# The opening of a two-layer hybrid diffusion backbone on one NeuronCore: another order of loads, statistic and modulation vectors, and three smaller moves

## What is computed

```
mx = split(silu(c)     @ ada_w[l] + ada_b[l], 9)     # shift, scale, gate for 3 sub-layers
mc = split(silu(c_ctx) @ ada_w[l] + ada_b[l], 9)
def ffn_sublayer(t, shift, scale, gate, g_pre, g_post, w_in, w_out):
    y = swiglu(rms_norm(t, g_pre) * (1 + scale) + shift, w_in, w_out)
    return t + 0.5 * gate * rms_norm(y, g_post)
lam = exp(sum(dl[0]*dl[1])) - exp(sum(dl[2]*dl[3])) + lambda_init     # used by attention a
kv  = rms_norm(parts[7]) @ w_ukv;  q = rms_norm(parts[6]) @ w_uq      # the norms of the latents
```

## Time and profile before

| | before |
|---|---|
| median of 3 runs | 2849.93 us |
| the profiled execution: its time | 2852.55 us |
| the profiled execution: its span | 2850.5 us |
| PE busy | 2737.2 us, 96% of the span |
| DVE / ACT / POOL busy | 61% / 44% / 9% |
| mean granted TensorE clock | 0.982 |

### The profile page before, as it was taken

The page is one execution under the profiler, slowest core; times in us unless marked ns, Lnnn a source line. Parts: engine busy times, 40 slices in busy tenths (PEclk is TensorE's granted clock), DMA queues, the critical chain, the costliest instruction groups (busy, mean ns, idle before and its releaser), DMA issues.

```text
span 2850.5 us, 42837 instructions
## 1 busy us (share of the span) xinstructions
PE 2737.2 (96%) x15754; PEld 2295.3 (81%) x15754; DVE 1743.1 (61%) x2907; ACT 1251.5 (44%) x2227; POOL 248.6 (9%) x342
## 2 busy tenths in 40 slices
PE   6999999999889999999999999999999989998997
PEld 4888898886666776788888898888988677877997
DVE  5677456656745443358676386772778766636754
ACT  2222355226545534446322354223553556555443
POOL 0000000111210000011000000100102120001000
PEclk8999999999999999999999999999999989999999
DMA  6555357431111121145555355553565222414654
GB/s 235 172 189 199 107 155 244 133 103 38 38 45 39 59 76 61 47 153 171 163 190 171 113 174 185 188 193 96 172 199 190 77 75 68 144 60 148 235 173 130
DMA packets 106643, 385.48 MB, mean 135 GB/s; under 512 B 12289, under 2 KB 14081, under 8 KB 104193
## 3 DMA queue, kind: packets, MB, share of 16 engines
q1 hardware_dynamic: 86370, 303.82, 33.1%
q0 software_dynamic: 20128, 79.70, 8.5%
HBM read 379.27 MB, written 4.20 MB: 135 GB/s over the span
## 4 chain that ended last, share of the span: by engine, by line
PE 85%; DVE 9%; ACT 3%; issue 2%; DMA 1%; POOL 0%; SPq 0%; POOLq 0%; DVEq 0%; ACTq 0%
PE ps L1934 24%; PE ps L1935 23%; PE ps L1942 23%; PE ps L917 3%; PE ps L896 3%; PE ps L879 2%; DVE wlo L1474 2%; PE ps L1998 1%; PE ps L2000 1%; PE ps L1995 1%; PE ps L869 1%; DVE mx L767 1%; ACT prob L683 1%; PE ps L875 1%; DVE work L1633 1%
## 5 line engine op out<-in xcount | busy, mean ns | idle before, releaser
L1474 DVE TENSOR_TENSOR wlo<-raw,whi 128x1024 fp32r<-128x1024 f32 x572 | 695.0, 1223 | 444.1 <-ACT whi L1166 443.4
L1934 PE MATMUL ps<-xhi,whi 128*128 128x512 f32 (+1 forms) x2432 | 827.8, 354 | 16.3 <-DVE xlo L1643 16.3
L1935 PE MATMUL ps<-xlo,whi 128*128 128x512 f32 (+1 forms) x2432 | 818.8, 351 | 0.0
L1166 ACT ACTIVATE whi<-raw 128x1024 fp32r<-128x1024 f32 x572 | 604.7, 1057 | 484.6 <-PE ps L1942 444.8
L1934 PEld LDWEIGHTS ps<-xhi,whi 128*128 128x128 f32 x2432 | 466.4, 192 | 85.5 <-DVE xlo L1643 18.6
L1935 PEld LDWEIGHTS ps<-xlo,whi 128*128 128x128 f32 x2432 | 467.3, 192 | 57.1
L1942 PE MATMUL ps<-xhi,wlo 128*128 128x512 f32 (+1 forms) x2432 | 509.8, 352 | 0.0
L1942 PEld LDWEIGHTS ps<-xhi,wlo 128*128 128x128 f32 x2432 | 403.7, 192 | 58.2 <-issue 0.7
L1710 DVE SCALAR_TENSOR_TENSOR work<-ada,work 128x1024 f32<-128x1024 f32 x256 | 299.4, 1220 | 2.1 <-DMA ada<-in_ada_rows 2.0
L1934 PE MATMUL ps<-ghi,whi 128*128 128x256 f32 (+1 forms) x968 | 279.0, 315 | 1.9 <-ACT whi L1166 1.9
L1935 PE MATMUL ps<-glo,whi 128*128 128x256 f32 (+1 forms) x968 | 277.9, 313 | 0.0
(11 more groups left out here) (209 smaller groups left out, 3322.9 us busy)
## 6 DMA issues: line engine op xcount, KB each, us to landing
raw<-in_ffn_in SPq DMA_DIRECT2D x192, 512.0 KB, 4.8
ada<-in_ada_rows POOLq DMA_DIRECT2D x128, 512.0 KB, 4.5
raw<-in_merge SPq DMA_DIRECT2D x96, 512.0 KB, 3.7
raw<-in_ffn_out SPq DMA_DIRECT2D x88, 512.0 KB, 3.6
raw<-in_ffn_out SPq DMA_DIRECT2D x44, 384.0 KB, 3.2
raw<-in_v_a SPq DMA_DIRECT2D x32, 512.0 KB, 4.4
raw<-in_qk_a SPq DMA_DIRECT2D x32, 512.0 KB, 3.7
raw<-in_wo SPq DMA_DIRECT2D x24, 512.0 KB, 4.0
```

What stands on the lines that cost most here:

```text
L1166: act.activation(whi[:, g.ring(SPLIT), :], raw[:, g.ring(RAW), :], ACT.Copy).then_inc(hi_ready, 1)
L1474: dve.tensor_tensor(wlo[:, g.ring(SPLIT), :], raw[:, g.ring(RAW), :], whi[:, g.ring(SPLIT), :].bitcast(F32), ALU.subtract).then_inc(lo_rea ...
L1934: pe.matmul(o, w, hi[:, first + c, ph.span], start=start, stop=False)
L1935: pe.matmul(o, w, lo[:, first + c, ph.span], start=False, stop=False)
```

## The change

1. **Loads.** Scale weights come in eight pieces, `x` in two. The order on SP is scale 0, 1, shift pair 0, scale 2, 3, half of `x`, scale 4, half of `x`, scale 5 to 7, biases and norm weights, the store of the conditioning rows, shift pairs 1 to 3, weight groups. Eight small constants and the two `ada` blocks are issued by POOL, once the last shift pair has landed.
2. **PE.** One shift pair goes ahead of the statistic, three behind it, each pair into a bank of its own. The lambda product moves to the start of the first output phase.
3. **DVE.** The newton steps follow the scale vector at once; each shift pair gets its bias when it is due (`shift_biased`); the low part of group 0 stands behind the first two `scaled`; the small constants stand behind the last `xlo`. ACT makes `whi` of group 0 behind the inverse root.
4. **Attention a.** POOL multiplies all tiles of a block with one tensor_tensor whose second operand is broadcast. The norm of the latents is spread over all eight tiles of the gate, one DVE segment a tile.
5. **The end.** The last norm uses the four instructions of the half norms (128x4x256), and each half of the output is sent as soon as it is there.

```diff
@@ pool_attention
-                    for t in range(nq // P):
-                        part = yraw[:, b % 2, t * P:(t + 1) * P]
-                        last = pool.tensor_scalar(part, part, yfac[:, b % 2, t:t + 1], None, ALU.mult)
-                    last.then_inc(done["yscaled"], 1)
+                    rows = nq // P
+                    part = yraw[:, b % 2, 0:nq].rearrange("p (t c) -> p t c", t=rows)
+                    factors = yfac[:, b % 2, 0:rows].unsqueeze(2).to_broadcast([P, rows, P])
+                    pool.tensor_tensor(part, part, factors, ALU.mult).then_inc(done["yscaled"], 1)
@@ sync
+            load_scale_w(0)
+            load_scale_w(1)
             load_shift_w(0)
+            load_scale_w(2)
+            load_scale_w(3)
+            load_x(0)
+            load_scale_w(4)
+            load_x(1)
+            for block in range(5, KC):
+                load_scale_w(block)
+            sp.dma_start(ada_b[:, :, :, :, :], io["ada_b"]).then_inc(biases_loaded, 16)
+            sp.dma_start(norm_g[:, :, :, :, :], io["norm_g"]).then_inc(biases_loaded, 16)
+            sp.wait_ge(silu_rows_made, 2)
+            sp.dma_start(silu_rows, c_all[0:1, :]).then_inc(silu_rows_stored, 16)
+            for pair in range(1, KC // ADA_PAIR):
                 load_shift_w(pair)
...
-            sp.wait_ge(done["x"], residual(plan[-1], KC - 1))
-            sp.dma_start(out, x[:, :, 0:S]).then_inc(stored, 16)
-            sp.wait_ge(stored, 16)
+            for b in range(BATCHES):
+                some = slice(b * KC // BATCHES, (b + 1) * KC // BATCHES)
+                sp.wait_ge(done["x"], base(plan[-1], "x") + b + 1)
+                sp.dma_start(out[:, some, :], x[:, some, 0:S]).then_inc(stored, 16)
+            sp.wait_ge(stored, 16 * BATCHES)
@@ gpsimd
+            pool.wait_ge(shift_w_loaded[-1], 16)
+            small = [(dlam, "dlam"), (subg, "subg"), (lat_g, "lat_g"), (cos, "cos"), (sin, "sin"), (ident, "ident"),
+                     (mask, "mask")]
+            for dst, name in small:
+                pool.dma_start(dst[tuple([slice(None)] * len(dst.shape))], io[name]).then_inc(consts_loaded, 16)
@@ latents_high (ACT)
+                for tile in range(HEAD):
+                    yield
+                    c = {2: 0, 3: 1, 4: 2, 5: 3, 6: 4}.get(tile)
+                    if c is not None:
...
                     yield
@@ scalar, norm
+                        inverse(STAT, ph.span, D, base(ph, "xsum") + KC, "xsum")
                         if not ph.post:
                             split_hi(Idx(0, 0, 0))
-                        inverse(STAT, ph.span, D, base(ph, "xsum") + KC, "xsum")
                         for c in range(KC):
+                            if not ph.post:
+                                act.wait_ge(shifts_made, c // ADA_PAIR + 1)
                             normed_high(ph, c)
@@ vector
+            def shift_biased(pair):
+
+                some = slice(pair * ADA_PAIR, (pair + 1) * ADA_PAIR)
+                dve.wait_ge(first_shift, pair + 1)
+                src = ps[:, SHIFT_BANKS[pair], 0:2 * ADA_PAIR].rearrange("p (c n) -> p c n", n=2)
+                dve.tensor_tensor(mods[:, 0, 0, some, :], src, ada_b[:, 0, 0, some, :], ALU.add)\
+                   .then_inc(shifts_made, 1)
+
+            def small_constants():
+
+                dve.wait_ge(consts_loaded, 128)
...
+                        if not ph.pre:
+                            for b in range(BATCHES):
+                                residual_added(ph, b)
+                            continue
...
                     if ph.pre:
+                        newton(step, dve, base(ph, "inv") + (2 if ph.post else 1), STAT, ph.span, D)
                         if not ph.post:
-                            split_lo(Idx(0, 0, 0))
-                        newton(step, dve, base(ph, "inv") + (2 if ph.post else 1), STAT, ph.span, D)
+                            dve.wait_ge(silu_rows_stored, 16)
                         scaled(ph, 0)
                         scaled(ph, 1)
+                        if not ph.post:
+                            shift_biased(0)
+                            split_lo(Idx(0, 0, 0))
                         for c in range(KC):
                             if c + 2 < KC:
                                 scaled(ph, c + 2)
+                                if not ph.post and c % ADA_PAIR == 0:
+                                    shift_biased(c // ADA_PAIR + 1)
+                            if not ph.post:
+                                dve.wait_ge(shifts_made, c // ADA_PAIR + 1)
                             normed_low(ph, c)
@@ tensor
-                        shift_products(range(KC - ADA_PAIR))
+                        shift_products(range(ADA_PAIR))
...
-                        shift_products(range(KC - ADA_PAIR, KC))
+                        for first in range(ADA_PAIR, KC, ADA_PAIR):
+                            shift_products(range(first, first + ADA_PAIR))
```

124 lines of the change are left out of this document (62 added, 62 removed).

## The result

The changed kernel takes 2816.53 us (median of 4 runs, 2812.94 to 2820.38), the kernel before 2852.31 on the same chip: a ratio of 0.988, 95% interval 0.9865 to 0.9896. That is 35.8 us, where 29.5 were forecast. The profiled execution took 2812.94 us, its span is 2811.3; against the span of before the gain is 39.2.

What follows compares the result with a forecast made beforehand. PE, busy 2737 of 2850.5 us, bounds the kernel; the opening is bound by bytes, then DVE. Gains 19.8 + 2.0 + 4 + 4 - 0.3 = 29.5 us gave a forecast of 2820 us, own range 2812 to 2828.

Steps and rivals of the forecast that it cites:

- The loads came in the queue's order: Opening: loads served in queue order, shift pair 0 landing at 10.6 us; rival that order fails, 2835 us, chance 0.03.
- DVE's path: Opening: newton at 28.8 us against 51.85, last `xlo` at 46.3 us, 21.2 us earlier.
- The pairs: Opening, PE: three shift pairs behind the statistic take 3.6, 5.3 and 7.0 us, ending at 43.3.
- The shift pairs are late next, not DVE: Opening: PE's first 16 passes end at 50.2 us, DVE alone would allow 47.2; opening gains 19.8 us.
- The constants: Opening: small constants from POOL land about 45.7 us, wanted at 46.3, cost 0; rival of late constants 2879 us, chance 0.01.
- The end: Last norm and output: four longer instructions and two output transfers gain 2.0 us, bounds 0.5 and 2.2.
- GpSimd's step: Attention a, POOL: one two-input instruction of 1.35 us replaces 3.4 us a block; gain 4 us, at most about 6, worst -5.
- The rival of the held-up DVE: Attention a: GpSimd's longer instruction holds up DVE, attention gives nothing or loses; 2830 us, chance 0.20.
- The latents' norm: Attention a: spreading it over eight gate tiles gains 4 us, a sixth of 27 us lost; bounds -3 and 12.
- the 0.3 for the lambda product: First output phase, PE: the moved lambda product stands between two full phases and costs 0.3 us.
- the four terms: Predicted gains: opening 19.8, end 2.0, attention a's POOL step 4 and latents' norm 4 us.
- everything fits: Rival: DVE's path decides the opening and attention gives 15 us; 2811 us, chance 0.13.

Runs made afterwards that it cites:

- u_both: Changed kernel with both attention a edits undone (POOL's single instruction per block, the spread of the latents' norm): 2829.99 us, ratio 0.9928 to the kernel before.
- u_pool: Changed kernel with GpSimd's edit undone, a block's tiles again multiplied in four (layer 1: two) one-input instructions: 2823.39 us, ratio 0.9911 to the kernel before.
- x_warmlo: Changed kernel with six products added among shift pairs 1 to 3 and group 0's low part moved to GpSimd: 2817.02 us, ratio 0.9900 to the kernel before.
- x_warm: Changed kernel with six added 128x256 products, two in each of shift pairs 1 to 3: 2819.80 us, ratio 0.9907 to the kernel before.

## Why the prediction was right, and where it was not

**The loads came in the queue's order: right.** They were about 1.1 us later than counted from the first shift pair on (11.7 instead of 10.6). The sums began at 7.7 instead of 7.4 and waited once, 1.26 us instead of 0.6, so newton began at 29.76 instead of 28.8.

**DVE's path: right.** Newton to the last `xlo` took 18.1 us; 15.65 + 1.2 + 0.7 = 17.55 were counted, and the wait for pair 3 is the other half microsecond.

**The pairs: right, one by one.** They took 3.63, 5.32 and 6.96 us, where 3.6, 5.3 and 7.0 were taken; with their overlaps that is 15.64 in all. They were meant to end at 43.3 and did at 43.7. The clock dropped at 33.4 us, inside the second, as assumed. That the profiled execution hit 5.32 is in part luck: in `u_both` the drop came at 31.2 and the same pairs ended at 46.5.

**"The shift pairs are late next, not DVE": right by 0.9 us, not by the 3 between 50.2 and 47.2.** All 16 passes were put at 0.43 us; the clock came back at 47 us, after eight of them, and the rest took 0.23 (chain above). Low passes from 48.95 instead of 50.2, while DVE was 1.6 us later than predicted, which took up most of the slack. The opening gave 20.6 us; the forecast was 19.8. Over the seven profiles with this opening the first `yinv` of layer 0 comes at 649.3 to 653.1 us, against 670.0 and 670.8 in the two with the old one, so the gain is 17 to 21.5 us and 19.8 lies inside.

**The constants: right.** No wait at 47.81.

**The end: 2.4 us, predicted 2.0 and at most 2.2.** DVE's part was as said. The output's second half took less time than the rows for transfers of 512 KB gave: the span ends 3.4 us behind the end of DVE's last instruction (2807.9), issue included.

**GpSimd's step: the mechanism right, the size not.** 4 us were taken, within -5 and 6; undoing it costs 7 to 9. "At most about 6 of the 7.5" held for the direct wait (5.8), and PE's idle time as a whole moves by 3.4, near the 4; but the term left out the clock, PE's busy time being 3.2 us higher in `u_pool`. One wait of 2.1 us was left, where none over 1.5 was foreseen. The instruction took 1.04 us in seven of the eight blocks of layer 0 (1.35 predicted) and 0.61 to 1.67 in layer 1. Two-input instructions of the same shape without a broadcast take 1.27 us at the least, so a broadcast operand has no price here. The Trainium skill's GPSIMD Engine Reference (4.1, Engine selection) would have had the two-input form cost more; against it stand 1.04 us for 128x512 in one instruction and 2.35 to 3.97 for four one-input ones in `u_pool`.

**The rival of the held-up DVE: there, but small.** DVE is busy 88.84 us in attention a of layer 0 with the one instruction, 86.59 with the four; in layer 1 56.85 against 55.13. That is 4 us of DVE in all, not 17. The two `ya` sums of 1.34 us that gave the price are there before and after, beside GpSimd's `yalo` and not beside this step; the change added one of 0.70. PE waited for GpSimd in one place only: its instruction took 1.95 us beside a low part, and PE waited 2.1. What can happen shows in `x_warmlo`: 0.88 to 4.04 us. SBUF — State Buffer of the Trainium skill (Who interferes with whom) has a port pair held for a whole instruction, by the engine that issues first. The row agrees in part: DVE's step ended only 0.3 us behind GpSimd's instruction, but by the records DVE had begun first, and its loss of 3.2 us is more than that instruction's 2.37. No run explains the difference.

**The latents' norm: mis-sized.** 4 us taken, 7 to 9 measured, within -3 and 12. I had the clock's 3.4 and 6.8 us in the sum of losses and then took a sixth of it all. The clock doesn't come back by sixths: in layer 0 the mean goes from 0.96 to 0.99 with both edits.

**Not in the sum at all: 2.8 us behind attention a of layer 0**, where the clock was at 0.88 and is now at 1.00. `u_both` has the stretch again (448.15 us to the next table load), and the kernels with one of the two edits don't (445.54 and 445.39). But that isn't proof that the edits decide it, for `x_warm` has both edits and the stretch too, 448.17 us to the next table load:

```profile
783.82:813.20 29.38, 25.53 (x139) 16.78 (x138) 16.89 (x44) 15.88 (x44) 0.00 (x0) 0.88 0.06 18
```

The nine other profiles with both edits have 445.4 to 445.6. So the stretch is rare with them, not gone.

This is part of the 13.5 us. So the forecast was 6.3 us short, and nearly all of it is attention a: 5.5 us there (13.5 against 8), 0.8 in the opening, 0.4 at the end. With the 0.3 for the lambda product, which no run isolates (its two records on PE take 0.38 us), the four terms add up to 36.2 for the 35.8 measured. They come from medians and from single profiles, so that they close to 0.4 us is more than they can promise. The chance of 0.13 for "everything fits" with 15 us from attention was too low; its other half, that DVE decides the opening, is nearly so.

## What to carry to other kernels

Where TensorE waits often for a little, price a wait at what it lasts and at the half clock that went with it here, and look for that behind the place too: of the 13.1 us of the two stretches 6.3 were waiting. Take the waiting from the engine's idle time and not from single rows of waits, which add up to more (10.2), since a wait removed in one row partly comes back in another. And look at several executions: the waiting repeated to 0.1 us, the half clock didn't. When two engines are to be balanced, compute both paths with the same clock, since a few microseconds of it decide which one is late. Work moved to an idle GpSimd isn't free for VectorE beside it: measure the neighbour, not only the step moved.
